# Modulation columns of a diffusion backbone: sixteen on TensorE beside the filter, the others as VectorE products inside the merges

## What is computed

```python
mod_l = jax.nn.silu(c) @ mod_w[l] + mod_b[l]            # mod_w[l]: 1024 x 6144
mod_c = jax.nn.silu(c_ctx) @ mod_w[l] + mod_b[l]
sh1, sc1, g1, sh2, sc2, g2 = jnp.split(mod_l[:, None, :], 6, axis=-1)
hl = _modulate(_rmsnorm(xl, norm1_g[l]), sh1, sc1)      # xn * (1 + scale) + shift
...                                                     # hyena, attention, mLSTM
mix_l = _merge(ym_l, ya_l, yh_l, pl[11], merge_b[l], w_br_m[l], w_br_a[l], w_br_h[l], w_out[l])
xl = xl + g1 * mix_l
tok = _modulate(_rmsnorm(xl, norm2_g[l]), sh2, sc2).reshape(B * L, D)
f = _moe(tok, router_w, router_b, e_w1[l], e_w3[l], e_w2[l])
xl = xl + g2 * f[:B * L].reshape(B, L, D)
```

## Time and profile before

| | us |
|---|---|
| median of 3 runs (3824.39 to 3825.43) | 3825.38 |
| the profiled execution | 3828.61 |
| its span in the profile | 3826.8 |
| TensorE busy | 3313.3 |
| VectorE busy | 1881.4 |
| ScalarE busy | 1543.5 |
| DMA | 611.66 MB, mean 160 GB/s |

### The profile page before, as it was taken

One profiled execution on the slowest core, in us unless ns is written; L12 is line 12 of the kernel. 1 busy time (PEld: TensorE's weight loads), 2 busy tenths in 40 slices (PEclk: granted clock), 3 DMA queues, 4 the chain that ended last, 5 costly groups with the idle time before them and its releaser, 6 DMA issues. The chain is left out here.

```text
span 3826.8 us, 49445 instructions
## 1 busy us (share of the span) xinstructions
PE 3313.3 (87%) x18110; PEld 2760.4 (72%) x18110; DVE 1881.4 (49%) x2724; ACT 1543.5 (40%) x2163; POOL 0.2 (0%) x4
## 2 busy tenths in 40 slices
PE   9979888987799697699999987878877878699998
PEld 9947676665577476388888854876666768599997
DVE  0054434553345433266666625544544444588884
ACT  0041133443233223166666614234433334477673
POOL 0000000000000000000000000000000000000000
PEclk9989999997899897899999998989978988799999
DMA  8711021102121022099999811231122214499994
GB/s 329 265 64 56 22 89 63 50 22 77 49 78 55 22 88 95 11 348 340 338 338 341 323 36 66 88 118 53 52 77 83 88 39 175 175 423 422 423 422 189
DMA packets 73724, 611.66 MB, mean 160 GB/s; under 512 B 9422, under 2 KB 11408, under 8 KB 12944
## 3 DMA queue, kind: packets, MB, share of 16 engines
q1 hardware_dynamic: 73616, 610.23, 41.8%
HBM read 609.15 MB, written 1.05 MB: 159 GB/s over the span
## 5 line engine op out<-in xcount | busy, mean ns | idle before, releaser
L152 PE MATMUL ps<-rounded,rounded 128*128 128x256 f32 (+1 forms) x1936 | 674.8, 349 | 111.4 <-DVE rounded L143 95.8
L153 PE MATMUL ps<-rounded,rounded 128*128 128x256 f32 (+1 forms) x1936 | 663.6, 343 | 0.0
L154 PE MATMUL ps<-rounded,rounded 128*128 128x256 f32 (+1 forms) x1936 | 662.0, 342 | 0.0
L143 DVE TENSOR_TENSOR rounded<-low_arena,rounded 128x1024 fp32r<-128x1024 f32 (+3 forms) x296 | 358.5, 1249 | 357.3 <-ACT rounded L139 357.3
L152 PEld LDWEIGHTS ps<-rounded,rounded 128*128 128x128 f32 x1936 | 384.7, 199 | 159.3 <-DVE rounded L143 93.3
L128 PE MATMUL ps<-high_arena 128*128 128x256 f32 (+3 forms) x1424 | 430.3, 462 | 72.9 <-ACT low_arena L1521 16.2
L128 PEld LDWEIGHTS ps<-low_arena,high_arena 128*128 128x128 f32 x4096 | 467.0, 192 | 7.4 <-issue 2.4
L128 PE MATMUL ps<-low_arena,high_arena 128*128 128x128 f32 x4096 | 467.7, 275 | 2.0 <-ACT low_arena L2125 1.3
L139 ACT ACTIVATE rounded<-low_arena 128x1024 fp32r<-128x1024 f32 (+3 forms) x296 | 305.9, 1074 | 326.9 <-PE ps L154 260.7
L128 PEld LDWEIGHTS ps<-high_arena 128*128 128x128 f32 x1424 | 282.1, 208 | 208.7 <-issue 114.7
L154 PEld LDWEIGHTS ps<-rounded,rounded 128*128 128x128 f32 x1936 | 383.7, 198 | 38.1
(11 more groups left out here) (307 smaller groups left out, 3721.8 us busy)
## 6 DMA issues: line engine op xcount, KB each, us to landing
high_arena<-in_e_w SPq DMA_DIRECT2D x248, 1024.0 KB, 7.3
high_arena<-in_e_w SPq DMA_DIRECT2D x68, 2048.0 KB, 9.1
low_arena<-in_d_modw SPq DMA_DIRECT2D x32, 1536.0 KB, 7.4
low_arena<-in_d_wm SPq DMA_DIRECT2D x48, 1024.0 KB, 4.8
low_arena<-in_d_wml SPq DMA_DIRECT2D x32, 1024.0 KB, 4.9
low_arena<-in_d_wh SPq DMA_DIRECT2D x16, 1536.0 KB, 6.6
low_arena<-in_d_wa SPq DMA_DIRECT2D x16, 1536.0 KB, 6.5
low_arena<-in_d_wo SPq DMA_DIRECT2D x8, 1024.0 KB, 4.8
```

Of the source, the lines that this page charges most:

```text
L143: return v.tensor_tensor(lo, raw, hi.bitcast(F32), ALU.subtract)
L152: pe.matmul(out, l_hi, r_hi, start=(k == 0), stop=False)
L153: pe.matmul(out, l_lo, r_hi, start=False, stop=False)
L154: last = pe.matmul(out, l_hi, r_lo, start=False, stop=(k == n - 1))
```

## The change

`stage_modulation` is gone. In its place stands `stage_constants`, which issues the DMAs of the constants, of x and of four tiles of `d_modfirst` (2 MB each, 4 columns of 128) and waits for two small ones. The 16 columns of the first norm of layer 0 are computed on TensorE inside `stage_norm_filter` of layer 0, with 16 copies of silu per stream instead of 48, so that a matmul is 128x32; the tiles stand between the matmuls of the filter.

The other 80 columns are computed in the five merges up to branch 1 of layer 1, two columns per output tile. `d_modlater` holds mod_w transposed: a partition is an output channel, and 1024 values along the row are multiplied by silu of the condition, which lies on all partitions (`d_cond`), and summed by VectorE (`accum_out`): four products a tile in layer 0 (two columns, two streams), two in layer 1. SP loads a modulation tile of 1 MB for each output tile. The selection matrix `d_sel` is now loaded in the gates stage, since the condition takes its place.

```diff
 def stage_norm_filter(nc, K, l):
@@ tensor
+            def modulate(u):
+                K.first.wait(pe, 1 + u)
+                w = first_mod_tile(K, u)[0].rearrange("p (k c) -> p k c", k=KC)
+                for c in range(FIRST_CH):
+                    last = accumulate(pe, mod_out[:, u * FIRST_CH + c, :], lambda k: w[:, k, c * P:c * P + P],
+                                      lambda k: sil[:, k, :], KC)
+                last.then_inc(modulated, 1)
...
 def stage_merge(nc, K, l, branch, first):
...
+        mod_tiles = KC if l == 0 or order < 2 else 0
+        mod_from = order * KC + 24 * l
@@ sync
             def load(u, s):
                 sp.dma_start(*merge_tile(K, l, branch, u, s)).then_inc(tile_in[s], 16)
+                if mod_tiles:
+                    sp.wait_ge(modulated, (u - 1) * 2 * ns)
+                    sp.dma_start(*later_mod_tile(K, u + mod_from, s)).then_inc(mod_in[s], 16)
+            if mod_tiles:
+                sp.dma_start(cond, K.A["d_cond"][:, streams[0]:, :]).then_inc(cond_in, 16)
+                for s in range(2):
+                    sp.dma_start(*later_mod_tile(K, mod_from + s, s)).then_inc(mod_in[s], 16)
...
-            prefetch(sp, KC, load, lambda u: sp.wait_ge(w_split, u + 1), K.early, tile_in)
+            for s in range(2):
+                K.early.hand_over(sp, s, tile_in[s])
+            for u in range(2, KC):
+                sp.wait_ge(w_split, u - 1)
+                load(u, u % 2)
@@ vector
+            def modulate(u, s):
+                v.wait_ge(mod_in[s], u // 2 * 16 + 16)
+                v.wait_ge(modulated, u * 2 * ns)
+                w = later_mod_tile(K, 0, s)[0].rearrange("p (c n) -> p c n", c=2)
+                for c in range(2):
+                    for i, st in enumerate(streams):
+                        products = w[:, c, :] if i else K.ps[:, 4 + 2 * c:6 + 2 * c, :].rearrange("p b n -> p (b n)")
+                        v.scalar_tensor_tensor(out=products, in0=w[:, c, :], scalar=0.5, in1=cond[:, i, :], op0=ALU.mult, op1=ALU.mult,
+                                               accum_out=K.mod[:, G1 + 2 * (mod_from + u) + c, st:st + 1]).then_inc(modulated, 1)
...
+                if mod_tiles:
+                    modulate(u, s)
-            with v.Fori(0, KC // 2 - 1) as i:
-                for s in range(2):
-                    unit(i * 2 + s, s)
-            for s in range(2):
-                unit(KC - 2 + s, s, more=False)
+            for u in range(KC):
+                unit(u, u % 2, more=u < KC - 2)
```

More of the change, by code:

```diff
@@ L89, in hand_over, with __init__, issue, wait @@
         sp.sem_inc(sem, 16)
+class Transfers:
+    def __init__(self, nc, name, n):
+        self.sems = [nc.alloc_semaphore(f"{name}{i}") for i in range(n)]
+        self.counts = [0] * n
+    def issue(self, sp, i, dst, src):
+        sp.dma_start(dst, src).then_inc(self.sems[i], 16)
+        self.counts[i] += 16
+    def wait(self, eng, i):
+        eng.wait_ge(self.sems[i], self.counts[i])
 class Chain:
@@ L185, in spans, with stage_constants @@
 def spans(l):
     return (0, 2) if l < DEPTH - 1 else (SEQ, 1)
[L190 to L207, removed]
+def stage_constants(nc, K):
+    names = ("constants_in", "ones_set")
+    with stage(nc, *names) as (constants_in, ones_set), nc.Block() as block:
@@ L209, in _ @@
         @block.sync
         def _(sp):
[L211 to L218, removed]
+            K.first.issue(sp, 0, K.f(163, KC * 2), K.A["cT"])
@@ L223, in _ @@
[L223 to L234, removed]
+                K.first.issue(sp, 6, dst, src)
@@ L236, in _ @@
+            sp.wait_ge(constants_in, 32)
         @block.vector
         def _(v):
[L238 to L243, removed]
@@ L269, in _ @@
[L269 to L284, removed]
+            v.wait_ge(ones_set, 2 + DEPTH)
@@ L343, in stage_norm_filter @@
         zT, w1, w2, neg_t, w3, delta, _ = (dst for dst, _ in filter_consts(K, l))
-        delta_step = 10
+        delta_step = 19 if first else 10
         total = K.ps[:, 7, :]
@@ L463, in _, with square @@
         def _(act):
-            for k in range(KC):
-                act.activation(K.H[:, k, :], K.X[:, k, :], ACT.Square).then_inc(x_squared, 1)
+            def square():
+                for k in range(KC):
+                    act.activation(K.H[:, k, :], K.X[:, k, :], ACT.Square).then_inc(x_squared, 1)
+            if first:
+                K.first.wait(act, 0)
+                act.activation(th, cT, ACT.Tanh, scale=0.5).then_inc(tanh_done, 1)
+            else:
+                square()
             for i in range(2):
@@ L468, in _ @@
                 act.activation(hid[i], arg, ACT.Sin).then_inc(sin_done, 1)
+                if first and i == 0:
+                    K.first.wait(act, 5)
+                    square()
             act.wait_ge(meaned, 1)
```

162 lines of the change are left out of this document (120 added, 42 removed).

## The result

| | before | changed |
|---|---|---|
| median, us | 3824.9 (3823.4 to 3825.4, 4 runs) | 3894.3 (3885.7 to 3901.8, 4 runs) |
| span of the profiled run, us | 3826.8 | 3892.4 |
| ratio, 95% interval | 1 | 1.0181 (1.0160 to 1.0203) |

The changed kernel is 1.8% slower. The forecast was 3913 us with a range of 3855 to 3950: the sign and the place were right, the loss was 65.6 us by the spans where 87.5 were forecast.

What follows compares the result with a forecast made beforehand. TensorE, busy 87% of the span, was taken to bound the kernel and its merges. First stages -118.5, merges +196 and small costs +10 gave +87.5 us, so 3913 us, range 3855 to 3950.

Steps and rivals of the forecast that it cites:

- The start: First stages: modulation stage's 186.8 us removed, filter stage over at 132 us instead of 250.5; 118.5 us gained (112 to 155).
- The holding of SP: Constants stage: SP, held by its issues behind large transfers, gets through its list at 28 us (bounds 11 and 32).
- tiles 1 to 3: Filter stage, narrow modulation matmuls: 12 us each for the two behind 512 column matmuls, 13.9 for the last.
- Tile 0: Filter stage, first tile of narrow modulation matmuls, after idle time: 13.9 us at the slow clock.
- The ring: Merges: SP's wait makes landing, rounding, split, products follow one another; 17.3 us a tile in layer 0, 14.6 in layer 1.
- the small costs: Three more DMAs ahead of hand-overs (6 us), more semaphores to clear (3), biases and gains at merge ends (1); together 10.
- The last unit: Last output tile of a layer 0 merge: 13.3 us on TensorE, running like a first one after six idle us.
- Outside the start and the merges: All other stages: nearly unchanged, +1 us.
- the merges absorb the products: Rival: weight tiles come in time, VectorE's work shows only in last units, 20 us in all; 3737 us, chance 0.12.
- The comparison of engines: Merges: leaving SP out, VectorE's some 7.6 us of idle time per layer 0 tile holds the 5.1 us of products.
- Half rate products: Rival: VectorE's products in the merges take 2.3 us each, 124 us more over five merges; 4037 us, chance 0.06.
- The rival of the faster clock in the first tiles: Rival: the filter stage's modulation tiles take 7.3 us each, 24 us less; 3889 us, chance 0.11.

Runs made afterwards that it cites:

- e1: Changed kernel with SP issuing merge weight tiles ahead of the wait for products, modulation tiles behind with waits of their own; 3731.7 us, 0.976 of before.
- e7: e4 with 64 columns instead of 32 in the filter stage's modulation tiles (32 copies of silu per stream, not 16); 3693.5 us, 0.9656 of before.
- e8: Kernel before the change, its modulation stage's matmuls cut from 96 to 32 columns, same 1536 records; 3981.0 us in one run.
- e4: Changed kernel with both e1's issue order in the merges and e3's later issues at the start; 3708.3 us, 0.9689 of before.
- e3: Changed kernel with seven small constants and two hyena tiles issued behind the hand-over in the filter stage, not ahead of it; 3867.7 us, 1.0115 of before.

## Why the prediction was right, and where it was off

**The start: -118.5 forecast, -118.2 measured, by two errors that cancelled.** The holding of SP was right in kind and size: it left the constants stage at 27.5 us where 28 was forecast from the earlier trace rows. What the step missed is what SP does next. It issues two hyena tiles ahead of the hand-over while the large transfers are still under way, and that held it for 9.34 us more. (A slip that changes little: the large transfers are 8.4 + 2.1 + 2.6 = 13.1 MB and not 12.6, by which the forecast's own rate gives 29 and not 28.) The other way, tiles 1 to 3 were forecast at 12 + 12 + 13.9 us and took 8.49 + 22.41, 7.0 less: the clock was still at 1.00 behind wide matmuls and fell only within the tile, where the forecast had put a mean of 0.82 on them. Tile 0 was right (13.86 for 13.9). That the sum came out within 0.3 us is luck.

**The ring: right, 17.3 forecast, 16.4 measured in layer 0; 14.6 and 14.1 in layer 1.** Where it adds, 16.6 to 17.2 for 17.5. The steps in layer 0: from SP's release to the landing 0.37 + 6.9 = 7.3, as forecast; rounding 1.91, as forecast; split and merge step 2.54 together for 2.68; products 1.147 each and 4.6 together for 5.1; the semaphores some 0.1 for 0.3. So the term that was mis-sized is the product, taken at 1.28. The five merges came to +190.9 for 195.7. In that figure the small costs that they carry (more semaphores to clear, three more issues, the last products) are contained, 9 of the 10 us that the forecast had for them; so against 204.7 the ring was over-sized by some 14 us, up to 0.9 us a turn in layer 0 and 0.5 in layer 1. That is the larger part of the error of 22 us. The last unit, forecast at 13.3 us from the end of its split to its gate in layer 0, took 11.7, 13.6 and 14.2.

**Outside the start and the merges: +1 forecast, -7.1 measured.** The other third of the error. The long expert stages ran a few us shorter than before (the last one 607.5 us for 612.2). In layer 0 they took 778.2 for 780.5. In both layers the two kernels that keep the modulation stage of before are the longest (612.2 and 612.3 in the last stage, 780.5 and 782.6 in layer 0), and the eight with the change lie below them (606.8 to 611.0, and 774.4 to 778.5), though no line of these stages was changed. Among the eight there is no order by what was edited. The cause stays open.

**The rivals.** That the merges absorb the products (3737 forecast for the changed kernel) failed for it, but is what happens once the wait stands behind the load: e1 gave 3731.7. The comparison of engines was right about the work and said nothing about the queue. Half rate products (4037) fell with the pitch of 1.147 us: the statement of the Trainium skill in "Vector Engine (DVE) Microarchitecture Reference", "Points that are easy to get wrong", does not hold for this form with an f32 output, two f32 sources in SBUF and a running sum. The rival of the faster clock in the first tiles (3889, the nearest to the time measured; its own terms give 22.6 us and not 24) was half true: the first tile did not run fast, but those behind wide matmuls began fast, which is 7.0 us. That it lies nearest is luck, since the start came out as forecast and the error lay in the ring and behind it.

**The signs named ahead.** Gates 17.3 apart: 16.4. VectorE idle before the split, released by ScalarE: 8.62 us. Weight tiles issued right behind a modulation tile: 0.37 us behind. Filter stage over at 132: the first transfer that SP issues in the hyena stage goes out at 141.49, where it was 259.95 before, 118.5 us sooner, so 132. Narrow matmuls 0.217 apart: for tile 0 and the second half of the others only.

## What to carry to other kernels

When work is put into a stage where an engine has idle time, compare also the order in which the in-order DMA queue issues: a wait placed ahead of the next load turns latencies that overlapped into a sum, and here the order of three lines was worth 165 us while the work itself, with the small costs of the stages, cost some 28. Where two transfers go out together, the one that is on the path goes first (65 us). And a transfer that nobody waits for is not free to issue ahead of a hand-over while large transfers are under way: here such issues held the whole kernel back by 27 us.

## What was not expected of the hardware

- The running sum of scalar_tensor_tensor costs VectorE nothing that can be seen: 1.147 us from one product of 128x1024 to the next, and the read of the accumulator (0.08 to 0.14 us) lies beside the next product.
- A record of these f32 matmuls takes nearly the same time at 32, 64 or 96 columns. At the upper level: 0.106 us (32 columns, 36 in 3.80 us), 0.113 (64, e7's tile 1) and 0.114 (96). At the pitch of the lower one: 0.2135 (32, e8), 0.217 (64, e7's tile 0) and 0.216 (96, the first 25 records of the kernel before, in 5.40 us). Fewer columns saved nothing here, and the runs differ in what the clock did. In the kernel before, the pitch fell from 0.216 to 0.122 us within the first 12 us of TensorE's work; in e8, with a third of the columns, it stayed at 0.2135 for 328 us. Behind 512 column matmuls e4's tiles of 32 fell to 0.50 and e7's of 64 stayed at 1.00, while e7's first one stayed at the lower pitch for all of its 13.88 us.
- From the start of a program the granted clock in the trace is not to be trusted: it reads 1.00 over e8's 328 us and over tile 0 of the changed kernel, both at the pitch of the lower level. This is inferred from the distance between records, which is the safer sign there.
- SP is held by the issues themselves: 9.73 us by that of one small constant and 9.34 by those of two tiles, behind 13 MB that stand ahead of them in its list. Issued from 31.23 us on, behind the hand-over (e3), the same two tiles take 1.19 us and the constants 0.42 to 0.58, but for the last with 3.92, and nobody waits for it. What exactly holds SP, a limit of the queue or something else, no run shows.
